# Block 1's softmax attention: two heads of a pair per step, on halves of the TensorE array

## Chip, cores and metric

One core of one Trainium2 chip. The metric is the device time of one launch in microseconds (us); the median of three runs is compared. All data are float32; TensorE runs each float32 matmul as two passes (so the trace counts two for each).

## What is computed

Two transformer-like blocks for 512 tokens of width 1024, then a final norm. Block 1 has two attentions of 8 heads with 64 dimensions each, sigmoid gates, a projection, an output product, and a product-key expert layer that gathers 128 expert rows per token. The change is in the first of these attentions:

```python
def dsa_attention(q, k, v, qi, ki, wi, rel_bias):
    ...
        score = jnp.einsum('bths,bth->bts', rel, wib).astype(jnp.float32) * idx_scale
        ...
        top_score, idx = lax.top_k(score, topk)
        ...
        logits = jnp.einsum('bthd,btkhd->bhtk', qb, kg).astype(jnp.float32) * (dh ** -0.5)
        bias = rel_bias[t5_bucket(q_pos[None, :, None] - idx)].astype(jnp.float32)
        logits = logits + jnp.moveaxis(bias, -1, 1)
        logits = jnp.where(valid[:, None], logits, -jnp.inf)
        p = jax.nn.softmax(logits, axis=-1).astype(v.dtype)
        return jnp.einsum('bhtk,btkhd->bthd', p, vg)
...
merged = jax.nn.sigmoid(ga) * (ya @ w_proj_a[l]) + jax.nn.sigmoid(gb) * (yb @ w_proj_b[l])
```

The kernel does not gather the chosen keys: it keeps all keys up to the query tile and adds a mask (`mask`) for the ones that were not chosen. By then the masks exist, as do q, k and v.

## The kernel before

Every engine has a program of its own, written out by hand, and runs it strictly in order; the engines wait for each other through counting semaphores. A `Signal` has `ready(n)` (item n is done) and `free(n, depth)` (item n - depth is done, so that its place can be used again). No planner orders this part; the order is that of the loops.

Block 1 runs in stages: norm, the q/k products, index scores, the second (stick-breaking) attention with the top-k masks beside it, and then the stage of this change. In it the softmax attention and the 16 gate products are woven into each other. A **unit** n is one head h = n // 4 and one query tile i = n % 4 of 128 tokens, with i + 1 key tiles of 128; there are 32. The gate products are 16 tiles (`S_GATE`) of 24 TensorE products each (lines 627 to 629: the high and low halves of a float32 product, 8 times 3); half a tile goes with each unit.

For a unit, in order:
- TensorE `scores` (L773): queries times keys, 64 rows of the array (rows 0 to 63 for even heads, 64 to 127 for odd), into bank 2 or 3. It waits (`s_taken`) until VectorE has taken the unit that used the bank before.
- VectorE (L1880) adds the bias rows and writes to one of three `logit` buffers; it waits first until the transposes of unit n - 3 have read that buffer (`t_done`). Then L1882 adds the mask and reduces to the row's extreme, and signals `s_taken`.
- ScalarE `exponents` (L1314), VectorE reciprocal of the sum (L1885), ScalarE `normalize` (L1320).
- TensorE `transposes` (L789), one per key tile, into bank 4 or 5; ScalarE `copy_turned` (L1332) copies them to `probT`.
- TensorE `values` (L799), one matmul per key tile, accumulated in a 64-column half of bank 6 or 7.
- When a pair of heads is complete, VectorE copies its y (L1777, L1779) and signals `y_taken`, for which the projection waits.

TensorE's loop (L805 to 813) issues in iteration n: scores(n+1), half a gate tile, transposes(n-1), values(n-2). ScalarE also copies each finished gate tile (L1325) and rounds the weight tile after next (L1202, `high`); VectorE makes that tile's low part (L1743, `low`). SP refills the ring of four weight tiles (L570) whenever TensorE has finished one. The projection (L816 on) starts only after the last y is taken.

Of the kernel before, what the change touches and what calls it, by code (L numbers as in the profile page):

```python
# [4 lines left out]
P = 128  # L5
D = 1024
KT = D // P
T = 512
TT = T // P
META = 16  # L10
L2 = META + T
NH, DH = 8, 64
HP = NH // 2
# [23 lines left out]
S_QK, S_KI, S_WI, S_V, S_GATE = 0, 20, 21, 22, 30  # L37
# [183 lines left out]
def program(nc, xT, metaT, cond, w_ada, small, onehot, rel_bias, w_stream, sub_keys, experts, outT):  # L221
    f32, u32, f32r = mybir.dt.float32, mybir.dt.uint32, mybir.dt.float32r
    ALU, ACT, AX = mybir.AluOpType, mybir.ActivationFunctionType, mybir.AxisListType.X
# [3 lines left out]
    with ctx:  # L227
# [32 lines left out]
        ident = sb("ident", [P, P])  # L260
# [9 lines left out]
        sq = sb("sq", [P, 2, L2])  # L270
        rstd = sb("rstd", [P, L2])
        col = sb("col", [P, 16])
# [39 lines left out]
        masks_at = used[0]  # L312
        mask = [take(P * (i + 1)) for i in range(TT)]
        probT = [take(TT, P) for _ in range(2)]
        logit = [sq[:, 0, 0:T], sq[:, 1, 0:T], take(T)]
        wi_rows = sq[0:NH, 0, 0:T]
        work = used[0]
        bias_rows = take(NH, T)
# [88 lines left out]
        def bank(b, width=512, start=0):  # L407
            return psum[:, b * 512 + start:b * 512 + start + width]
# [202 lines left out]
        def _(pe):  # L611
# [151 lines left out]
                weighted(m)  # L763


            def unit(n):
                return n // TT, n % TT

            def scores(n):
                h, i = unit(n)  # L770
                r = slice(64 * (h % 2), 64 * (h % 2) + 64)
                pe.wait_ge(s_taken.sem, s_taken.free(n, 2))
                mm(bank(2 + n % 2, P * (i + 1)), qk[r, QA + h // 2, i * P:(i + 1) * P],  # L773
                   qk[r, KA + h // 2, 0:P * (i + 1)], start=True, stop=True).then_inc(s_done.sem, 1)

            def half_gate(n):
                g, part_of = n // 2, n % 2
# [7 lines left out]
            def transposes(n):  # L785
                pe.wait_ge(p_done.sem, p_done.ready(n))
                pe.wait_ge(t_taken.sem, t_taken.free(n, 2))
                for j in range(unit(n)[1] + 1):
                    last = nc.tensor.transpose(bank(4 + n % 2, P, j * P), logit[n % 3][:, j * P:(j + 1) * P], ident[:])  # L789
                last.then_inc(t_done.sem, 1)  # L790

            def values(n):
                h, i = unit(n)
                q, e = h // 2, h % 2
                if n % (2 * TT) == 0:
                    pe.wait_ge(y_taken.sem, y_taken.free(q, 2))
                pe.wait_ge(t_taken.sem, t_taken.ready(n))
                for j in range(i + 1):
                    last = mm(bank(6 + q % 2, P, i * P)[64 * e:64 * e + 64, :], v[:, j, h * DH:(h + 1) * DH],  # L799
                              probT[n % 2][:, j, :], start=j == 0, stop=j == i)  # L800
                last.then_inc(pv_done.sem, 1)

            pe.wait_ge(yb_taken.sem, yb_taken.ready(HP - 1))
            scores(0)
            for n in range(NH * TT + 2):  # L805
                if n + 1 < NH * TT:
                    scores(n + 1)
                if n < NH * TT:
                    half_gate(n)
                if 1 <= n <= NH * TT:  # L810
                    transposes(n - 1)
                if n >= 2:
                    values(n - 2)


            pe.wait_ge(y_taken.sem, y_taken.ready(HP - 1))  # L816
# [364 lines left out]
        def _(act):  # L1181
# [14 lines left out]
            def high(n):  # L1196

                act.wait_ge(ring_ready[n % SLOTS], 16 * (n // SLOTS + 1))
                same = n - (4 if S_V + 4 <= n < S_GATE + 2 else 2)
                if same >= 0 and not S_V + 2 <= n < S_V + 4:  # L1200
                    act.wait_ge(tile_done.sem, tile_done.ready(same))
                op(rounded(n), ring[:, n % SLOTS, :], ACT.Copy).then_inc(w_rounded.sem, 1)  # L1202
# [102 lines left out]
                    soft_side(m + 1)  # L1305
                weights(m, 3)

            def unit(n):
                return n // TT, n % TT

            def exponents(n):
                w = P * (unit(n)[1] + 1)
                act.wait_ge(s_taken.sem, s_taken.ready(n))
                op(logit[n % 3][:, 0:w], logit[n % 3][:, 0:w], ACT.Exp, scale=-1.0, bias=col[:, n % 3:n % 3 + 1],  # L1314
                   accum_out=col[:, 3 + n % 3:4 + n % 3]).then_inc(exp_done.sem, 1)

            def normalize(n):
                w = P * (unit(n)[1] + 1)
                act.wait_ge(share_done.sem, share_done.ready(n))
                op(logit[n % 3][:, 0:w], logit[n % 3][:, 0:w], ACT.Copy, scale=col[:, 6 + n % 3:7 + n % 3])\  # L1320
                    .then_inc(p_done.sem, 1)

            def gate(g):
                act.wait_ge(tile_done.sem, tile_done.ready(S_GATE + g))
                op(gates[:, g, :], bank(g % 2), ACT.Copy).then_inc(dense_act.sem, 1)  # L1325

            def copy_turned(n):
                i = unit(n)[1]
                act.wait_ge(t_done.sem, t_done.ready(n))
                if n >= 2:  # L1330
                    act.wait_ge(pv_done.sem, pv_done.ready(n - 2))
                op(probT[n % 2][:, 0:i + 1, :], bank(4 + n % 2, P * (i + 1)).rearrange("p (a b) -> p a b", b=P),  # L1332
                   ACT.Copy).then_inc(t_taken.sem, 1)

            for n in range(NH * TT + 1):
                if n < NH * TT:
                    exponents(n)
                    normalize(n)
                if n % 2 == 1:
                    gate(n // 2)  # L1340
# [367 lines left out]
        def _(dve):  # L1708
# [160 lines left out]
            take_pair(HP - 1)  # L1869

            dve.wait_ge(bias_loaded, 16)
            for n in range(NH * TT + 2):
                if n < NH * TT:
                    h, i = n // TT, n % TT
                    w = P * (i + 1)
                    lg = logit[n % 3][:, 0:w]
# [5 lines left out]
                    V.tensor_tensor_reduce(out=lg, in0=lg, in1=mask[i], scale=1.0, scalar=-TAKEN, op0=ALU.add,  # L1882
                                           op1=ALU.min, accum_out=col[:, n % 3:n % 3 + 1]).then_inc(s_taken.sem, 1)
                    dve.wait_ge(exp_done.sem, exp_done.ready(n))
                    V.reciprocal(col[:, 6 + n % 3:7 + n % 3], col[:, 3 + n % 3:4 + n % 3]).then_inc(share_done.sem, 1)  # L1885
                if n >= 2 and n % 2 == 0:
                    low(S_GATE + n // 2 + 1)
                if n >= 9 and n % 8 == 1:
                    q = n // 8 - 1
                    dve.wait_ge(pv_done.sem, pv_done.ready(8 * q + 7))  # L1890
                    low_part(y_low[0][:, q, :], bank(6 + q % 2), y_high[0][:, q, :])
                    tell(dve, steps, y_taken)


# [373 lines left out]
```

## Time and profile before

| | us |
|---|---|
| median of 3 runs | 2556.46 (2549.74 to 2558.13) |
| the profiled execution: device time | 2555.75 |
| the profiled execution: span of the trace | 2553.8 |
| TensorE busy | 2147.7 (84%) |
| VectorE busy | 1340.0 (52%) |
| ScalarE busy | 932.8 (37%) |
| GpSimd busy | 592.7 (23%) |

In the rows, PE is TensorE, PEld its weight loads, DVE VectorE, ACT ScalarE, POOL GpSimd and SP SyncE; L773 is line 773. `DVEq` is VectorE's sequencer (a semaphore increment by an instruction of its own). PEclk is the TensorE clock that was granted, as a share of the full 2.4 GHz; 0.50 is 1.2 GHz. The span is the time from the first to the last instruction; the device time has some 2 us more around it. TensorE's matmuls are pipelined: the duration of one is longer than the distance to the next, so distances between starts tell what a matmul costs in a stream.

### The profile page before, as it was taken

To read this page: it belongs to the slowest core of one execution; us is meant where nothing else is said; L and a number is where in the kernel's file an instruction comes from. 1 tells how busy PE (TensorE), PEld (TensorE's weight loads), DVE (VectorE), ACT (ScalarE), POOL (GpSimd) and SP (SyncE) were. 2 spreads that over 40 slices of the span, in tenths; PEclk is the share of its full clock that TensorE was granted. 3 is DMA by queue.
4 is the path that set the end of the run, shared out by engine and by line. 5 is a ranking of instruction groups with operands and counts; after the bars stand their busy time and mean duration, and the time that the engine had idled before them with its cause. 6 is when DMAs were issued, how large, how long until landed. Compare 5 with 4: busy or idle time off the path is not lost.

```text
span 2553.8 us, 30169 instructions
## 1 busy us (share of the span) xinstructions
PE 2147.7 (84%) x10876; PEld 1309.5 (51%) x10876; DVE 1340.0 (52%) x3152; ACT 932.8 (37%) x2322; POOL 592.7 (23%) x568
## 2 busy tenths in 40 slices
PE   5999999998878655655566898899999878999999
PEld 3877567776634211111112543356666535668888
DVE  7743754354667777777778677754443342111000
ACT  3124434523334433333334558734443123421000
POOL 0000100000344444444443334433332220000000
PEclk9999999999989877787878998899999999889999
DMA  8821001122799999999999999999999992114454
GB/s 329 293 72 59 1 26 58 58 99 66 299 419 419 421 419 413 421 421 416 416 412 418 377 356 421 379 419 418 418 417 418 418 378 66 42 43 140 156 154 151
DMA packets 124272, 710.48 MB, mean 278 GB/s; under 512 B 14648, under 2 KB 16824, under 8 KB 58464
## 3 DMA queue, kind: packets, MB, share of 16 engines
q0 software_dynamic: 74432, 540.07, 51.5%
q1 hardware_dynamic: 49456, 168.38, 18.9%
q8 instruction: 83, 1.36, 0.2%
q14 instruction: 61, 0.50, 0.1%
q10 hardware_dynamic: 240, 0.16, 0.0%
HBM read 706.45 MB, written 2.12 MB: 277 GB/s over the span
## 4 chain that ended last, share of the span: by engine, by line
PE 57%; DMA 27%; DVE 6%; ACT 5%; issue 3%; POOL 2%; SPq 0%; ACTq 0%; POOLq 0%; DVEq 0%
DMA arena<-experts,eidx 26%; PE psum L1138 9%; PE psum L882 9%; PE psum L627 6%; PE psum L628 5%; PE psum L629 5%; DVE arena L1725 3%; PE psum L1151 3%; POOL arena L1700 2%; PE psum L1120 2%; PE psum L949 2%; PE psum L999 2%; PE psum L739 1%; ACT sq L1406 1%; PE psum L715 1%
## 5 line engine op out<-in xcount | busy, mean ns | idle before, releaser
L882 PE MATMUL psum<-arena,sq 64*64 64x512 f32 x4096 | 626.4, 737 | 333.6 <-ACT sq L1406 326.4
L1725 DVE CUSTOM_DVE_ANT_0 arena<-arena 128x1024 f32<-128x1024 f32 x560 | 679.5, 1223 | 390.9 <-DMA arena<-experts,eidx 360.7
L1700 POOL DMA_INDIRECT arena<-experts,eidx x512 | 577.8, 1128 | 963.8 <-PE psum L882 771.9
L882 PEld LDWEIGHTS psum<-arena,sq 64*64 64x64 f32 x4096 | 152.2, 153 | 725.8 <-ACT sq L1406 503.1
L1138 PE MATMUL psum<-n_t,ring 128*128 128x256 f32 x1408 | 313.9, 382 | 2.4 <-DVE n_t L1722 2.4
L1392 ACT ACTIVATE arena<-arena 128x2 f32<-128x2 f32 x256 | 52.0, 203 | 722.1 <-DVE arena L1725 720.7
L1138 PEld LDWEIGHTS psum<-n_t,ring 128*128 128x128 f32 x1408 | 264.3, 190 | 66.1 <-issue 30.5
L627 PE MATMUL psum<-hn_high,w_high 128*128 128x512 f32 (+1 forms) x432 | 178.6, 413 | 14.6 <-DVE hn_low L1722 13.3
L628 PE MATMUL psum<-hn_low,w_high 128*128 128x512 f32 (+1 forms) x432 | 173.3, 401 | 0.0
L629 PE MATMUL psum<-hn_high,ring_low 128*128 128x512 f32 (+1 forms) x432 | 172.1, 398 | 0.0
L1406 ACT ACTIVATE sq<-sq,arena 128x64 f32<-128x64 f32 x512 | 150.3, 340 | 24.9 <-ACT arena L1398 1.5
L1398 ACT ACTIVATE arena<-arena 128x1 f32<-128x1 f32 x512 | 122.9, 287 | 10.4
L1202 ACT ACTIVATE w_high<-ring 128x1024 fp32r<-128x1024 f32 x74 | 77.9, 1055 | 132.3 <-PE psum L629 130.8
L627 PEld LDWEIGHTS psum<-hn_high,w_high 128*128 128x128 f32 (+1 forms) x432 | 81.8, 189 | 62.3 <-issue 36.2
L1743 DVE TENSOR_TENSOR ring_low<-ring,w_high 128x1024 fp32r<-128x1024 f32 x74 | 90.1, 1219 | 39.4 <-ACT w_high L1202 37.8
L1392 ACT ACT_TABLE_LOAD x75 | 96.2, 1283 | 7.1 <-ACT hn_rest L1618 4.0
L629 PEld LDWEIGHTS psum<-hn_high,ring_low 128*128 128x128 f32 (+1 forms) x432 | 82.1, 190 | 20.0
L628 PEld LDWEIGHTS psum<-hn_low,w_high 128*128 128x128 f32 (+1 forms) x432 | 82.2, 190 | 17.3
L1689 POOL TENSOR_SCALAR_AFFINE_SELECT arena<-arena 128x128 f32<-128x128 f32 x32 | 9.3, 292 | 271.9 <-DVE arena L1722 271.5
L1618 ACT ACTIVATE hn_rest<-psum 128x256 f32<-128x256 f32 x44 | 16.9, 383 | 143.2 <-PE psum L1138 142.9
L1120 PE MATMUL psum<-mix,ring 128*128 128x256 f32 x256 | 59.0, 390 | 2.1 <-ACTq L1502 2.1
L1151 PE MATMUL psum<-w_rest,ring 128*128 128x256 f32 x256 | 59.0, 381 | 0.0
(280 smaller groups left out, 2814.0 us busy)
## 6 DMA issues: line engine op xcount, KB each, us to landing
ring<-w_stream SPq DMA_DIRECT2D x264, 512.0 KB, 4.1
arena<-w_ada SPq DMA_DIRECT2D x48, 512.0 KB, 6.4
arena<-experts,eidx POOLq DMA_INDIRECT x512, 12.4
x<-xT SPq DMA_DIRECT2D x1, 2048.0 KB, 14.9
arena<-rel_rows POOLq DMA_DIRECT2D x1, 2048.0 KB, 15.0
outT<-hn_rest SPq DMA_DIRECT2D x16, 128.0 KB, 6.0
arena<-sub_keys POOLq DMA_DIRECT2D x1, 1024.0 KB, 6.3
arena<-cond SPq DMA_DIRECT2D x1, 512.0 KB, 4.4
```

The costliest lines, as they stand in the source:

```text
L627: mm(out, a[0], b[0], start=start, stop=False)
L628: mm(out, a[0], b[1], start=False, stop=False)
L629: return mm(out, a[1], b[0], start=False, stop=stop)
L882: last = mm(bank(4 + 2 * odd + a)[HALF * b:HALF * b + HALF, :], diag[k, s, :], rows[k, s, D + a * 512:D + (a + 1) * 512], start=c == 0, st ...
L1120: last = mm(bank(b, PAIR), w[:, k, :], mix[:, k, :], start=k == 0, stop=k == KT - 1)
L1138: last = mm(bank(b, PAIR), w[:, k, :], n_t[:, k, 0:PAIR], start=k == 0, stop=k == KT - 1)
L1151: last = mm(bank(b, PAIR), w[:, f % 8, :], act_ff[f], start=f == 0, stop=f == FF - 1)
L1392: steps(op(pre[:, s:s + 2], pre[:, s:s + 2], ACT.Gelu))
L1398: steps(op(coef[:, s + c:s + c + 1], pre[:, s + c:s + c + 1], ACT.Copy, scale=wgt[:, n // P % 2, k:k + 1]))
L1406: op(diag[:, s + c, :], ident_pair, ACT.Copy, scale=coef[:, s + c:s + c + 1]).then_inc(diag_done.sem, 1)
L1700: nc.gpsimd.indirect_dma_start(rows[:, s, :], None, experts, bass.IndirectOffsetOnAxis(ap=eidx[:, n // P % 2, n % P:n % P + 1], axis=0)).t ...
L1725: return V.tensor_tensor_reduce(out=out, in0=a, in1=b, scale=1.0, scalar=0.0 if op1 == ALU.add else TAKEN, op0=op0, op1=op1, accum_out=accum)
```

## The change

A **step** s now is one pair of heads q = s // 4 and one query tile i = s % 4, so two units, 2s (even head) and 2s + 1 (odd head); there are 16 steps. TensorE issues the two scores matmuls one after the other, on rows 0 to 63 and 64 to 127 of the array and into banks 2 and 3, and alternates the values of the two heads, which go to columns 0 to 63 and 64 to 127. Each step has a whole gate tile, in two halves with the values between them. The order within an iteration is scores(s+1), first half of the gate tile, values(s-2), second half, transposes(s-1). There are four `logit` buffers in place of three, and the small columns beside them move accordingly. ScalarE and VectorE do the two units of a step one after the other, operation by operation.

```diff
-        logit = [sq[:, 0, 0:T], sq[:, 1, 0:T], take(T)]
+        logit = [sq[:, 0, 0:T], sq[:, 1, 0:T], take(T), take(T)]
...
-            def scores(n):
-                h, i = unit(n)
-                r = slice(64 * (h % 2), 64 * (h % 2) + 64)
-                pe.wait_ge(s_taken.sem, s_taken.free(n, 2))
-                mm(bank(2 + n % 2, P * (i + 1)), qk[r, QA + h // 2, i * P:(i + 1) * P],
-                   qk[r, KA + h // 2, 0:P * (i + 1)], start=True, stop=True).then_inc(s_done.sem, 1)
+            def scores(s):
+                q, i = s // TT, s % TT
+                pe.wait_ge(s_taken.sem, s_taken.free(2 * s + 1, 2))
+                for e in range(2):
+                    r = slice(64 * e, 64 * e + 64)
+                    mm(bank(2 + e, P * (i + 1)), qk[r, QA + q, i * P:(i + 1) * P], qk[r, KA + q, 0:P * (i + 1)],
+                       start=True, stop=True).then_inc(s_done.sem, 1)
...
+            def transposes(s):
+                for e in range(2):
+                    n = 2 * s + e
+                    pe.wait_ge(p_done.sem, p_done.ready(n))
+                    pe.wait_ge(t_taken.sem, t_taken.free(n, 2))
+                    for j in range(s % TT + 1):
+                        last = nc.tensor.transpose(bank(4 + e, P, j * P), logit[n % 4][:, j * P:(j + 1) * P], ident[:])
+                    last.then_inc(t_done.sem, 1)
+
+            def values(s):
+                q, i = s // TT, s % TT
+                if i == 0:
                     pe.wait_ge(y_taken.sem, y_taken.free(q, 2))
+                pe.wait_ge(t_taken.sem, t_taken.ready(2 * s + 1))
                 for j in range(i + 1):
+                    for e in range(2):
+                        h = 2 * q + e
+                        last = mm(bank(6 + q % 2, P, i * P)[64 * e:64 * e + 64, :], v[:, j, h * DH:(h + 1) * DH],
+                                  probT[e][:, j, :], start=j == 0, stop=j == i)
+                        if j == i:
+                            last.then_inc(pv_done.sem, 1)
...
             scores(0)
-            for n in range(NH * TT + 2):
-                if n + 1 < NH * TT:
-                    scores(n + 1)
-                if n < NH * TT:
-                    half_gate(n)
-                if 1 <= n <= NH * TT:
-                    transposes(n - 1)
-                if n >= 2:
-                    values(n - 2)
+            S = HP * TT
+            for s in range(S + 2):
+                if s + 1 < S:
+                    scores(s + 1)
+                if s < S:
+                    half_gate(s, 0)
+                if s >= 2:
+                    values(s - 2)
+                if s < S:
+                    half_gate(s, 1)
+                if 1 <= s <= S:
+                    transposes(s - 1)
```

On ScalarE:

```diff
-            for n in range(NH * TT + 1):
-                if n < NH * TT:
-                    exponents(n)
-                    normalize(n)
-                if n % 2 == 1:
-                    gate(n // 2)
-                if n >= 1:
-                    copy_turned(n - 1)
-                if n % 2 == 1:
-                    high(S_GATE + n // 2 + 2)
+            S = HP * TT
+            for s in range(S + 1):
+                if s < S:
+                    exponents(2 * s)
+                    exponents(2 * s + 1)
+                    normalize(2 * s)
+                    normalize(2 * s + 1)
+                    gate(s)
+                if s >= 1:
+                    copy_turned(2 * s - 2)
+                    copy_turned(2 * s - 1)
+                if s < S:
+                    high(S_GATE + s + 2)
```

On VectorE:

```diff
+            for s in range(S + 2):
+                q, i = s // TT, s % TT
+                w = P * (i + 1)
+                for n in (2 * s, 2 * s + 1) if s < S else ():
+                    lg = logit[n % 4][:, 0:w]
                     dve.wait_ge(s_done.sem, s_done.ready(n))
-                    if n >= 3:
-                        dve.wait_ge(t_done.sem, t_done.ready(n - 3))
-                    steps(V.tensor_tensor(lg, bank(2 + n % 2, w), bias_rows[:, h, 0:w][:, ::-1], ALU.add))
+                    if n >= 4:
+                        dve.wait_ge(t_done.sem, t_done.ready(n - 4))
+                    steps(V.tensor_tensor(lg, bank(2 + n % 2, w), bias_rows[:, 2 * q + n % 2, 0:w][:, ::-1], ALU.add))
                     steps.wait()
...
+                for n in (2 * s, 2 * s + 1) if s < S else ():
                     dve.wait_ge(exp_done.sem, exp_done.ready(n))
...
-                if n >= 2 and n % 2 == 0:
-                    low(S_GATE + n // 2 + 1)
+                if 1 <= s <= S:
+                    low(S_GATE + s + 1)
+                if s >= 5 and s % 4 == 1:
+                    y_of = s // 4 - 1
+                    dve.wait_ge(pv_done.sem, pv_done.ready(8 * y_of + 7))
```

## Rows read from the trace of the kernel before

**Rows 1.** The page, part 4: shares of the span in the chain that ended last.
```profile
PE 57%; DMA 27%; DVE 6%; ACT 5%; issue 3%; POOL 2%; SPq 0%; ACTq 0%; POOLq 0%; DVEq 0%
```

**Rows 2.** Windows, stage and four units: length; busy PE, PEld, DVE, ACT, POOL; PEclk; DMA; GB/s.
```profile
347.16:499.29 152.13, 150.04 (x689) 105.93 (x689) 58.47 (x152) 75.78 (x162) 0.00 (x0) 1.00 0.18 56
378.31:397.05 18.74, 18.74 (x88) 13.25 (x87) 6.33 (x17) 9.01 (x21) 0.00 (x0) 1.00 0.19 57
```

**Rows 3.** Chain that ended last, 405 to 412 us: start, length, what.
```profile
405.02 0.44 PE psum L789 x4
405.46 0.80 PE psum L799 x6
406.26 0.84 PE psum L773 x2
407.10 0.43 PE psum L627
408.23 0.24 PE psum L628
...
410.21 1.02 PE psum L799 x8
411.23 1.05 PE psum L773 x2
```

**Rows 4.** Timeline of TensorE, one expert combine: start, length; in brackets the idle time before.
```profile
2106.46 1.95 PE L882 MATMUL psum<-arena,sq 64*64 64x512 f32 x16 [1.64 <-ACT sq L1406]
```

**Rows 5.** Timeline of VectorE: first and last instruction of two units' taking.
```profile
399.69 0.29 DVE L1880 TENSOR_TENSOR sq<-psum,arena 128x128 f32<-128x128 f32 x1
400.23 0.08 DVE L1882 DVE_READ_ACCUMULATOR2_ANT col<- 128x1 f32 x1
...
413.68 0.68 DVE L1880 TENSOR_TENSOR sq<-psum,arena 128x512 f32<-128x512 f32 x1
...
415.01 0.08 DVE L1882 DVE_READ_ACCUMULATOR2_ANT col<- 128x1 f32 x1
```

**Rows 6.** Timeline of the end of the stage, from the last gate product on.
```profile
493.43 0.39 PE L629 MATMUL psum<-hn_high,ring_low 128*128 128x512 f32 x1
...
493.86 0.60 ACT L1325 ACTIVATE arena<-psum 128x512 f32<-128x512 f32 x1 [1.30 <-PE psum L629]
...
494.35 0.48 ACT L1332 ACTIVATE arena<-psum 128x384 f32<-128x384 f32 x1
...
497.45 0.69 DVE L1777 CAST ya_high<-psum 128x512 fp32r<-128x512 f32 x1 [0.41 <-PE psum L799]
...
499.29 0.49 PE L627 MATMUL psum<-ya_high,w_high 128*128 128x512 f32 x1 [1.88 <-DVEq L552]
```

**Rows 7.** Timeline: the stage's start, and three more pauses of TensorE.
```profile
347.16 0.92 PE L773 MATMUL psum<-arena 64*128 64x128 f32 x4 [1.64 <-DVEq L552]
347.76 0.29 DVE L1880 TENSOR_TENSOR sq<-psum,arena 128x128 f32<-128x128 f32 x1 [0.70 <-PE psum L773]
...
549.13 0.79 PE L627 MATMUL psum<-merged_high,w_high 128*128 128x512 f32 x1 [3.42 <-DVEq L552]
...
2126.05 3.69 PE L926 MATMUL psum<-n_t,mean_ones 128*128 128x256 f32 x16 [2.16 <-ACT n_t L1425]
...
2287.85 3.41 PE L1120 MATMUL psum<-mix,ring 128*128 128x256 f32 x9 [2.10 <-ACTq L1502]
```

**Rows 8.** Windows of TensorE around these pauses: length, PE busy, PEclk, DMA, GB/s.
```profile
345.50:352.50 7.00, 5.36 (x22) 1.00 0.00 0
497.40:504.40 7.00, 5.12 (x16) 0.76 0.00 0
545.70:552.70 7.00, 3.58 (x9) 0.65 0.65 226
2124.00:2131.00 7.00, 3.69 (x16) 1.00 0.00 0
2285.80:2292.80 7.00, 4.95 (x15) 0.76 0.25 75
```

More of the change, by code:

```diff
@@ L763, in _, with half_gate @@
                 weighted(m)
-            def unit(n):
-                return n // TT, n % TT
-            def scores(n):
-                h, i = unit(n)
-                r = slice(64 * (h % 2), 64 * (h % 2) + 64)
-                pe.wait_ge(s_taken.sem, s_taken.free(n, 2))
-                mm(bank(2 + n % 2, P * (i + 1)), qk[r, QA + h // 2, i * P:(i + 1) * P],
-                   qk[r, KA + h // 2, 0:P * (i + 1)], start=True, stop=True).then_inc(s_done.sem, 1)
-            def half_gate(n):
-                g, part_of = n // 2, n % 2
+            def scores(s):
[5 more added lines that the diff above has]
+                       start=True, stop=True).then_inc(s_done.sem, 1)
+            def half_gate(g, part_of):
                 w = tile(S_GATE, g)
@@ L783, in half_gate @@
                     last.then_inc(tile_done.sem, 1)
[L785 to L795, printed above, removed]
+            def transposes(s):
[6 more added lines that the diff above has]
+                    last.then_inc(t_done.sem, 1)
@@ L796, in values @@
+            def values(s):
+                q, i = s // TT, s % TT
+                if i == 0:
                     pe.wait_ge(y_taken.sem, y_taken.free(q, 2))
-                pe.wait_ge(t_taken.sem, t_taken.ready(n))
+                pe.wait_ge(t_taken.sem, t_taken.ready(2 * s + 1))
                 for j in range(i + 1):
-                    last = mm(bank(6 + q % 2, P, i * P)[64 * e:64 * e + 64, :], v[:, j, h * DH:(h + 1) * DH],
-                              probT[n % 2][:, j, :], start=j == 0, stop=j == i)
@@ L801, in values @@
-                last.then_inc(pv_done.sem, 1)
+                    for e in range(2):
[4 more added lines that the diff above has]
+                            last.then_inc(pv_done.sem, 1)
             pe.wait_ge(yb_taken.sem, yb_taken.ready(HP - 1))
             scores(0)
-            for n in range(NH * TT + 2):
-                if n + 1 < NH * TT:
-                    scores(n + 1)
-                if n < NH * TT:
-                    half_gate(n)
-                if 1 <= n <= NH * TT:
-                    transposes(n - 1)
-                if n >= 2:
-                    values(n - 2)
+            S = HP * TT
@@ L1306, in _ @@
                 weights(m, 3)
-            def unit(n):
-                return n // TT, n % TT
             def exponents(n):
-                w = P * (unit(n)[1] + 1)
+                w = P * (n // 2 % TT + 1)
                 act.wait_ge(s_taken.sem, s_taken.ready(n))
-                op(logit[n % 3][:, 0:w], logit[n % 3][:, 0:w], ACT.Exp, scale=-1.0, bias=col[:, n % 3:n % 3 + 1],
-                   accum_out=col[:, 3 + n % 3:4 + n % 3]).then_inc(exp_done.sem, 1)
+                op(logit[n % 4][:, 0:w], logit[n % 4][:, 0:w], ACT.Exp, scale=-1.0, bias=col[:, n % 4:n % 4 + 1],
+                   accum_out=col[:, 4 + n % 4:5 + n % 4]).then_inc(exp_done.sem, 1)
             def normalize(n):
-                w = P * (unit(n)[1] + 1)
+                w = P * (n // 2 % TT + 1)
                 act.wait_ge(share_done.sem, share_done.ready(n))
-                op(logit[n % 3][:, 0:w], logit[n % 3][:, 0:w], ACT.Copy, scale=col[:, 6 + n % 3:7 + n % 3])\
+                op(logit[n % 4][:, 0:w], logit[n % 4][:, 0:w], ACT.Copy, scale=col[:, 8 + n % 4:9 + n % 4])\
                     .then_inc(p_done.sem, 1)
@@ L1327, in copy_turned @@
             def copy_turned(n):
-                i = unit(n)[1]
+                i = n // 2 % TT
                 act.wait_ge(t_done.sem, t_done.ready(n))
@@ L1871, in _ @@
             dve.wait_ge(bias_loaded, 16)
[L1872 to L1876, printed above, removed]
+            S = HP * TT
+            for s in range(S + 2):
[3 more added lines that the diff above has]
+                    lg = logit[n % 4][:, 0:w]
                     dve.wait_ge(s_done.sem, s_done.ready(n))
-                    if n >= 3:
-                        dve.wait_ge(t_done.sem, t_done.ready(n - 3))
-                    steps(V.tensor_tensor(lg, bank(2 + n % 2, w), bias_rows[:, h, 0:w][:, ::-1], ALU.add))
+                    if n >= 4:
+                        dve.wait_ge(t_done.sem, t_done.ready(n - 4))
+                    steps(V.tensor_tensor(lg, bank(2 + n % 2, w), bias_rows[:, 2 * q + n % 2, 0:w][:, ::-1], ALU.add))
@@ L1881, in _ @@
                     steps.wait()
                     V.tensor_tensor_reduce(out=lg, in0=lg, in1=mask[i], scale=1.0, scalar=-TAKEN, op0=ALU.add,
-                                           op1=ALU.min, accum_out=col[:, n % 3:n % 3 + 1]).then_inc(s_taken.sem, 1)
+                                           op1=ALU.min, accum_out=col[:, n % 4:n % 4 + 1]).then_inc(s_taken.sem, 1)
+                for n in (2 * s, 2 * s + 1) if s < S else ():
                     dve.wait_ge(exp_done.sem, exp_done.ready(n))
-                    V.reciprocal(col[:, 6 + n % 3:7 + n % 3], col[:, 3 + n % 3:4 + n % 3]).then_inc(share_done.sem, 1)
@@ L1886, in _ @@
-                if n >= 2 and n % 2 == 0:
-                    low(S_GATE + n // 2 + 1)
[L1888 to L1891, printed above, removed]
+                    V.reciprocal(col[:, 8 + n % 4:9 + n % 4], col[:, 4 + n % 4:5 + n % 4]).then_inc(share_done.sem, 1)
+                if 1 <= s <= S:
+                    low(S_GATE + s + 1)
@@ L1892, in _ @@
+                if s >= 5 and s % 4 == 1:
+                    y_of = s // 4 - 1
+                    dve.wait_ge(pv_done.sem, pv_done.ready(8 * y_of + 7))
+                    low_part(y_low[0][:, y_of, :], bank(6 + y_of % 2), y_high[0][:, y_of, :])
                     tell(dve, steps, y_taken)
```

## The prediction

> **What bounds the kernel now.** I read the page first, then one stage of it, then the order of work inside that stage. The chain that ended last is TensorE for 57% of the span and DMA for 27% [rows 1]; the DMA share belongs to the expert gathers, which come later. The change touches one stage only, block 1's softmax attention, from the first scores matmul at 347.16 us to the first product of the projection at 499.29 us. In those 152.13 us TensorE is busy for 150.04 at full clock, VectorE for 58.47, ScalarE for 75.78 [rows 2]. So TensorE's own queue sets this stage; what it saves or waits there moves all that follows, because projection, queries and gathers each start on what came before. The other engines have room for their sums, but only if nobody in the queue has to wait for them.
>
> The stage holds 32 units (8 heads, 4 query tiles), of 1, 2, 3 and 4 key tiles in turn, and 16 gate tiles of 24 products. The chain prices a unit [rows 3]: a transposed tile 0.11 us (0.44 for four); values of three tiles 0.80 and of four 1.02, so 0.14 + 0.22 per tile; scores of three tiles 0.84 and of four 1.05, so 0.20 + 0.21 per tile; the first gate product behind a scores matmul 0.43 against 0.23 to 0.24 later, so 0.20 more. These small constants are what a change of the array's shape costs. A check: four units have 10 tiles each of transposes (1.10), values (2.76) and scores (2.92), 4 x 0.20 behind the scores, and 48 gate products of 0.2325 (11.16): 18.74 us, which is exactly the period from 378.31 to 397.05 [rows 2].
>
> **What the change saves on TensorE.** A step now handles both heads of a pair. The two scores matmuls use row halves 0 to 63 and 64 to 127 and write banks 2 and 3; the two chains of values use column halves. Before shows no such pair side by side in this stage. The nearest row is the expert combine, which puts 64 x 64 quarters side by side: 16 matmuls of 512 columns in 1.95 us at full clock [rows 4], where sixteen in a row at the 0.43 of a scores pass (0.85 for two) would need 6.8. That is all four quarters at work together. So I take a pair at the price of one, in full. The bounds are this and no overlap at all. Transposes stay as they are. Changes of shape fall: scores and values now each have gate products on both sides, which costs 2 x 0.20 per step behind them, where two units had 2 x 0.20 as well, while the 0.14 and 0.20 are paid once and not twice. Four steps (8 units) thus take 22.32 for gates, 2.20 for transposes, 2.76 for values, 2.92 for scores and 8 x 0.20: 31.80 us against 37.48. Over 16 steps that is **-22.7 us**. Without any overlap, 0.21 and 0.22 times 40 tiles come back (17.2 us), and -5.5 is left.
>
> The Trainium skill ("TensorE: Matmul & The Clock Gate", Part 3, The mechanism) says that matmuls start and end strictly in program order and overlap only across different tiles of the array. As each of these matmuls is two passes on the same tile, a pair would by that rule need three slots and not two for scores, and the sum would come out about 6 us higher. The combine's 1.95 us does not agree with it: with two passes in order on each quarter, at most two would run together.
>
> **What the change makes TensorE wait for.** VectorE turns a unit's scores into logits in two operations (L1880, L1882), and writes them into a logit buffer that must have been transposed. Before, three buffers for single units leave room: unit n waits for the transposes of unit n-3, issued an iteration or more before anybody needs the result. Now four buffers are two steps. Step s+1 writes where step s-1 was, and the transposes of step s-1 are the last thing in TensorE's iteration s. The first thing in iteration s+1 is scores(s+2), which waits until both units of step s+1 are taken from banks 2 and 3. So TensorE finishes the transposes, VectorE then does two adds and two reductions, and only then can TensorE go on. Both gate halves, the values and the next transposes stand behind that wait in the queue. Nothing covers it.
>
> Its size: one unit takes VectorE 0.62 us for one key tile (399.69 to 400.31) and 1.41 for four (413.68 to 415.09) [rows 5], so 0.62 + 0.263 per further tile. Two units with a gap of 0.05 take 1.29, 1.82, 2.34 and 2.87. From the end of a TensorE stream to the start of the engine that waits for it I take 0.20 (gate product 493.43 + 0.23, gate copy 493.86) [rows 6], and 0.05 back to TensorE. TensorE still streams the second head's transposes meanwhile, 0.11 per tile of step s-1 (3, 4, 1 and 2 tiles), and 0.10 of the scores' constant falls inside the wait. The waits are 1.29+0.25-0.33-0.10 = 1.11, 1.82+0.25-0.44-0.10 = 1.53, then 2.34+0.25-0.11-0.10 = 2.38, and 2.87+0.25-0.22-0.10 = 2.80 us for steps of 1, 2, 3 and 4 key tiles. They occur for VectorE's steps 3 to 15, in all 13: 4 x 2.80 + 3 x (1.11 + 1.53 + 2.38) = **+26.3 us**. This is the price of the operations alone; a late VectorE would add to it. I find no lateness: its reciprocals, its weight tile (1.2 us) and the y part (1.4 us) are done in the middle of TensorE's iteration.
>
> Smaller terms. At the start, scores(1) waits for both units of step 0; VectorE starts at 347.76 [rows 7], ends the pair at 349.05, TensorE goes on at 349.10 instead of 347.57: **+1.5**. At the end, before has 5.63 us from the last gate product (493.66) to 499.29, of which 3.2 are transposes and values: 2.5 bare. After: transposes(14), gate copy until +0.80, two copies of 0.48, values(14) until +2.6, transposes(15) until +3.6, two four-tile copies of 0.60 (the form of the gate copy) until +4.45, values(15) until +5.65, then the same 1.84 of VectorE and signal as from 497.45 to 499.29 [rows 6]: 7.5, of which 3.4 is TensorE's work, 4.1 bare: **+1.7**. ScalarE's exponents, normalisations and copies cost nothing more: after a wait it needs about 6 us to the last normalisation, TensorE comes to the next transposes after about 10. If that cover went, each us would be paid 13 times. SP's ring refills are released by the same gate tiles, 16 in some 150 us; POOL does nothing here. The sum at full clock is -22.7 + 26.3 + 1.5 + 1.7 = **+6.8 us**.
>
> **The clock.** The stage runs at 1.00 now, with no pause in it. The new pauses are 1.1 to 2.8 us long. Pauses of this length in the trace go both ways [rows 7, 8]: after 1.64 us (347.16) and 2.16 us (2126.05) the mean clock of the 7 us around stays 1.00; after 1.88 us (499.29) [rows 6] and 2.10 us (2287.85) it is 0.76; after 3.42 us it is 0.65. One fall to 1.2 GHz thus costs 0.24 x 7 = 1.7 us. I take six falls in thirteen, near the two of four: **+10.2 us**. The bounds are none (0) and all thirteen (+22). The tail's fall is there before and after.
>
> The Trainium skill ("TensorE: Matmul & The Clock Gate", Why this matters for your kernels) warns only of idle gaps longer than any that I expect here; by it none of these would cost clock and the forecast would be the second case below. The trace does not agree: the 1.88 us pause was followed by 0.76.
>
> **Forecast.** +6.8 + 10.2 = +17.0. Against the profiled execution's own 2555.75 us (span 2553.8) this is 2572.8; that execution lies 0.7 us under the median of the runs, 2556.46, so the median gives 2573.5. I say **2573 us, slower, chance 0.60**. A measurement can tell about 0.3%, 7.7 us, from no change.
>
> **The rivals.**
> Clock holds: the waits are as computed but the pauses cost no clock. +6.8, so 2563 us. For it: two pauses of four above. Chance 0.20, on the border of what can be told, so 0.13 goes to no change and 0.07 to slower.
> Pairs do not overlap: the halves run one after another, so that the change does not do what it says. 17.2 more than the forecast: 2590 us. Against it [rows 4]; for it, that no row has row halves or column halves alone. Chance 0.10, all slower; the in-order rule of the skill lies between the two.
> Faster: TensorE's wait for the two logit units decides. If VectorE takes the pair soon enough after the first head's transposes, the 22.7 us stay. The place is the head of iterations 2 to 14; the point from which it decides is a mean wait of (22.7 - 1.5 - 1.7) / 13 = 1.5 us with the clock up, against my 2.0. With no wait there at all the time would be 2556.5 - 19.5 = 2537 us. For it: TensorE saves more than in any other place of the stage, and VectorE is busy only 38% of it. Against it: the order of signals, in which no other work can slip in. Chance 0.10, of which 0.02 lands within 0.3%.
>
> **The numbers.** Faster 0.08, same 0.15, slower 0.77 (0.60 + 0.07 + 0.10). The range runs from under the clock-holds case, 2558, to the no-overlap case, 2591; it leaves out the faster case, and more than six falls on top of no overlap.
>
> **What would show it.** In the profile after: scores matmuls as groups of four with an idle time before them, put down to VectorE, 13 times, of 1.1 to 2.8 us by the step's width; a group of two three-tile scores at 0.84 and not 1.5; VectorE's add waiting for the transposes; the stage's length at 347 to about 523 us; its mean clock near 0.94 instead of 1.00. Wrong: no idle time before the scores, or a stage under 152 us; a paired scores group twice as long; a clock at 1.00.

## The result, and the profile after

The changed kernel takes 2566.9 us (median of 20 runs, 2555.94 to 2574.51), the kernel before 2554.77 (20 runs, 2544.61 to 2559.97): 12.1 us more, ratio 1.0049 with a 95% interval of 1.0037 to 1.0060. The profiled execution took 2571.63 us against 2555.75, 15.9 us more. It lies 4.7 us above its kernel's median. Single executions differ outside this stage too: in the nine profiles of this document the stage begins at 345.2 to 352.3 us, and what follows it, which is the same code in all, takes 2042.0 to 2058.0 us. So what the profiles are compared by below is the length of the stage.

The first view is the window of the stage, from its first scores matmul to the first product of the projection; the columns are those of [rows 2].

```profile
347.10:515.09 167.99, 138.77 (x689) 99.42 (x689) 58.76 (x152) 71.25 (x162) 0.00 (x0) 0.93 0.16 51
```
Against the 152.13 us of before [rows 2] the stage begins at the same time and is 15.9 us longer. From its end to the end of the span both kernels take the same (2569.7 - 515.09 = 2054.6, 2553.8 - 499.29 = 2054.5 us). So between these two executions all of the difference is here. VectorE and ScalarE are busy about as long as before (58.76 against 58.47 us, 71.25 against 75.78). TensorE is busy for 11 us less, idle for 27 us more, and its mean clock is 0.93 and no longer 1.00.

The second view is TensorE's timeline with what is idle before the scores of eight steps, and one group of values:

```profile
366.04 2.08 PE L771 MATMUL psum<-arena 64*128 64x512 f32 x4 [2.28 <-DVE col L1887]
378.19 0.49 PE L771 MATMUL psum<-arena 64*128 64x128 f32 x4 [2.71 <-DVE col L1887]
388.45 0.70 PE L771 MATMUL psum<-arena 64*128 64x256 f32 x4 [1.00 <-DVE col L1887]
398.24 0.92 PE L771 MATMUL psum<-arena 64*128 64x384 f32 x4 [1.42 <-DVE col L1887]
402.06 1.09 PE L799 MATMUL psum<-arena 128*64 128x128 f32 x16
408.67 1.13 PE L771 MATMUL psum<-arena 64*128 64x512 f32 x4 [2.28 <-DVE col L1887]
419.26 0.49 PE L771 MATMUL psum<-arena 64*128 64x128 f32 x4 [2.71 <-DVE col L1887]
...
483.29 0.92 PE L771 MATMUL psum<-arena 64*128 64x384 f32 x4 [1.42 <-DVE col L1887]
...
493.75 1.13 PE L771 MATMUL psum<-arena 64*128 64x512 f32 x4 [2.28 <-DVE col L1887]
```

The scores of a single unit of four key tiles in the kernel before, and a pair after, each with the gate product that follows:

```profile
411.16 1.12 PE L773 MATMUL psum<-arena 64*128 64x512 f32 x2
412.21 0.51 PE L627 MATMUL psum<-hn_high,w_high 128*128 128x512 f32 x1
...
449.76 1.13 PE L771 MATMUL psum<-arena 64*128 64x512 f32 x4 [2.28 <-DVE col L1887]
450.82 0.50 PE L627 MATMUL psum<-hn_high,w_high 128*128 128x512 f32 x1
```

Two things are to be seen. A scores pair of four key tiles (x4: two matmuls of two passes each) takes 1.13 us where a single unit had taken 1.12, and the gate product follows its start after 1.06 us, as against 1.05 before. Both heads' values of four key tiles, sixteen passes, take 1.09, as long as the eight of one head alone (e5 below). The halves of the array do work side by side. And ahead of each of the last thirteen scores pairs TensorE now stands idle for 1.0, 1.4, 2.3 or 2.7 us, released by VectorE. The waits within the stage add it up (us in total, times, longest):

```profile
DVE arena L1885 <- PE psum L788: 42.0, 7, 7.3
DVE sq L1885 <- PE psum L788: 30.3, 7, 8.2
PE psum L771 <- DVE col L1887: 25.8, 14, 2.7
```

VectorE's add (L1885) waits for the transposes (L788), TensorE's scores (L771) for VectorE's reduction (L1887). The chain shows one such turn, without anything between its links (start, length):

```profile
406.17 0.23 PE psum L788 x2
406.40 0.55 DVE sq L1885
...
407.46 0.08 DVE col L1887
407.54 0.48 DVE sq L1885
408.02 0.02 issue
408.05 0.56 DVE sq L1887
408.61 0.02 DVE col L1887
408.62 0.04 issue
408.67 1.13 PE psum L771 x4
```

The clock is seen in windows of TensorE (length, busy, PEclk, DMA, GB/s), the first two around the pause that ends at 366.04, the others around the one that ends at 378.19:

```profile
361.00:366.04 5.04, 2.76 (x13) 0.99 0.26 81
366.04:370.04 4.00, 4.00 (x10) 0.58 0.09 33
375.00:379.00 4.00, 1.29 (x11) 1.00 0.42 131
379.00:384.00 5.00, 5.00 (x21) 0.66 0.00 0
```

In the stage of this execution TensorE fell to 1.2 GHz six times, five times with a loss of 1.7 us of full-speed time and once of 3.2, 11.6 us in all (windows of 1 us, 1 - PEclk times TensorE's busy time, summed up). The first of the six comes right after the start of the stage, where a pause of 1.32 us follows one of 1.63:

```profile
347.06 0.49 PE L771 MATMUL psum<-arena 64*128 64x128 f32 x4 [1.63 <-DVEq L552]
348.87 1.22 PE L771 MATMUL psum<-arena 64*128 64x256 f32 x4 [1.32 <-DVE col L1887]
```

A fall right behind the stage is there in both kernels, at 500 us before and at 516 us after.

### The profile page after: what moved, and what is told of

It reads as the page before. It is cut to its first block, busy times and chain, and to the rows that moved or that the text cites. A ratio compares the mean times of both kernels' runs of the same rounds, so it can differ in the third digit from the quotient of the medians.

```text
span 2569.7 us, 30168 instructions
## 1 busy us (share of the span) xinstructions
PE 2134.7 (83%) x10876; PEld 1300.1 (51%) x10876; DVE 1340.0 (52%) x3152; ACT 928.4 (36%) x2322; POOL 597.1 (23%) x568
## 4 chain that ended last, share of the span: by engine, by line
PE 57%; DMA 26%; DVE 6%; ACT 6%; issue 3%; POOL 2%; ACTq 0%; SPq 0%; POOLq 0%; DVEq 0%
DMA arena<-experts,eidx 25%; PE psum L1142 10%; PE psum L886 9%; PE psum L627 6%; PE psum L628 5%; PE psum L629 5%; DVE arena L1729 3%; PE psum L1155 3%; POOL arena L1704 2%; PE psum L953 2%; PE psum L1003 2%; PE psum L1124 2%; PE psum L739 1%; ACT sq L1410 1%; PE psum L715 1%
## 5 line engine op out<-in xcount | busy, mean ns | idle before, releaser
L1124 PE MATMUL psum<-mix,ring 128*128 128x256 f32 x256 | 57.4, 382 | 2.1 <-ACTq L1506 2.1
L1155 PE MATMUL psum<-mix,ring 128*128 128x256 f32 x256 | 59.0, 381 | 0.0
```

Source lines behind the costliest of these rows:

```text
L1124: last = mm(bank(b, PAIR), w[:, k, :], mix[:, k, :], start=k == 0, stop=k == KT - 1)
L1155: last = mm(bank(b, PAIR), w[:, f % 8, :], act_ff[f], start=f == 0, stop=f == FF - 1)
```

## The experiments

**e1, six logit buffers.** The wait's reason is taken away and TensorE's order left alone. The sixth buffer is the place of the index keys, which nobody reads by then.

```diff
-        logit = [sq[:, 0, 0:T], sq[:, 1, 0:T], take(T), take(T)]
+        logit = [sq[:, 0, 0:T], sq[:, 1, 0:T], take(T), take(T), take(T), ki[:]]
...
-                    if n >= 4:
-                        dve.wait_ge(t_done.sem, t_done.ready(n - 4))
+                    if n >= 6:
+                        dve.wait_ge(t_done.sem, t_done.ready(n - 6))
```
(and `n % 6` for `n % 4` wherever `logit` is indexed)

> Edit: six logit buffers instead of four, so that VectorE's step s+1 waits for the transposes of step s-2 and no longer for those that TensorE has just issued; the order of TensorE's work is untouched. Theory (the wait for the logit buffers sets TensorE's pauses): the idle time before the scores matmuls, 25.8 us in 14 places after the change, falls under 4 us (what is left is at the start), the clock stays at 1.00 through the stage, the stage takes 168.0 - 24.5 - about 12 = 131 to 134 us against 152.1 before, and the kernel about 2536 us, ratio to before 0.992 to 0.994. Rival (pairing costs TensorE or ScalarE something of its own, for instance ScalarE comes late when it does two units at a time): pauses remain before transposes or values, the stage stays above 145 us and the kernel within 8 us of before.

Measured: 2533.0 us (4 runs), ratio 0.9914 (0.9892 to 0.9937). The profiled execution is the slowest of the four (2543.03), and its stage begins 5 us later than before's; only the stage is compared. It is:

```profile
352.30:488.23 135.93, 128.92 (x688) 93.67 (x689) 58.15 (x152) 70.45 (x162) 0.00 (x0) 0.99 0.20 63
```

32 us shorter than after the change, by the buffers alone. Ten of the thirteen pauses are gone. The one at the start stays (1.32 us, with one fall of the clock), and three of 0.75 to 0.77 us are left where VectorE takes a pair's y first:

```profile
397.68 0.69 DVE L1781 CAST ya_high<-psum 128x512 fp32r<-128x512 f32 x1 [0.97 <-PE psum L799]
...
398.40 0.69 DVE L1783 TENSOR_TENSOR ya_low<-psum,ya_high 128x512 fp32r<-128x512 f32 x1
...
399.31 0.56 DVE L1885 TENSOR_TENSOR sq<-psum,arena 128x384 f32<-128x384 f32 x1 [0.21 <-DVE ya_low L1783]
...
401.59 1.13 PE L771 MATMUL psum<-arena 64*128 64x512 f32 x4 [0.76 <-DVE col L1887]
```

VectorE waits 0.97 us for the values, does 1.4 us for y, and begins the step's adds late. My expectation of 131 to 134 us left these three and the fall out (2.3 and 1.7 us). The theory stands, and the rival that pairing costs something of its own falls.

**e2, scores behind the first half gate tile.** The wait stays, work is put over it.

```diff
+                if s < S:
+                    half_gate(s, 0)
                 if s + 1 < S:
                     scores(s + 1)
-                if s < S:
-                    half_gate(s, 0)
                 if s >= 2:
                     values(s - 2)
```

> Edit: in TensorE's iteration the first half of the gate tile goes ahead of scores(s+1); everything else as in the change. Theory: VectorE has the 2.8 us of the half tile to take the pair (it needs 1.0 to 2.7 beyond TensorE's own transposes), so that all 13 pauses go; scores directly ahead of values also save one change of the array's shape per step (about 0.2 us). Stage about 130 us, clock 1.00, kernel about 2533 us, ratio 0.991 to 0.993. Rival (the pauses only move: scores(s+1) issued 2.8 us later makes VectorE or ScalarE late for the transposes): idle time of over 10 us in the stage, put down to ScalarE, and a kernel time above 2545.

Measured: 2526.23 us (5 runs), ratio 0.9892 (0.9873 to 0.9911). The stage, and one scores pair and values within it:

```profile
345.30:473.36 128.06, 124.66 (x688) 92.11 (x689) 58.79 (x152) 71.28 (x162) 0.00 (x0) 1.00 0.22 66
```
```profile
400.61 0.49 PE L771 MATMUL psum<-arena 64*128 64x128 f32 x4
401.03 0.66 PE L799 MATMUL psum<-arena 128*64 128x128 f32 x8
```

No pause stands before any scores pair, no fall lies in the stage, and what idle time is left (3.4 us) is in the tail, behind ScalarE's copies and VectorE's y. The rival falls. This version beats both kernels, before by 1.1%. Part of that is not the pauses: the change's stage without its falls, the 24.5 us and the start's 1.3 would be 130.6 us, and 2.5 less are left here, with scores directly ahead of values (expected: about 0.2 us per step).

**e3, the pauses filled.** It takes the clock apart from the wait.

```diff
             for s in range(S + 2):
+                if 2 <= s < S - 1:
+                    w = tile(S_GATE, s)
+                    pe.wait_ge(dense_act.sem, dense_act.free(A_GATE + s, 2))
+                    for _ in range((4, 6, 9, 11)[s % 4]):
+                        mm(bank(s % 2), w[0][:, 0, :], rhs[0][:, 0, :], start=True, stop=True)
                 if s + 1 < S:
                     scores(s + 1)
```

> Edit: ahead of the scores of iterations 2 to 14 TensorE does 4, 6, 9 or 11 products of 128 x 512 that nobody reads, 0.93, 1.40, 2.10 and 2.56 us of work, as long as the pauses there (1.00, 1.42, 2.28, 2.71). Nothing else is computed otherwise. Theory (a third of the loss is the clock): the waits keep their end, so no us is gained on them, but the clock stays at 1.00 and the five falls inside the stage go: about 10 us less than the change, 2557 us, ratio to before about 1.001. Rival (the falls cost nothing on the path, or come from elsewhere): the kernel stays at 2567 us, ratio 1.005, with the same lower clock in the stage.

Measured: 2561.42 us (12 runs, 2553.11 to 2571.43), ratio 1.0029 (1.0016 to 1.0042). The stage:

```profile
347.80:506.71 158.91, 152.53 (x787) 111.01 (x788) 58.78 (x152) 71.30 (x162) 0.00 (x0) 0.99 0.17 54
```

The pauses shrink to 0.2 us at most. In the stage only the fall after the start is left, and the stage is 9.1 us shorter than in the change's first profile, 6.2 shorter than in its second (e7), though TensorE does 99 products more. The rival falls in the traces. Over the timed runs the gain is 5.5 us, about half of what I gave, but the two intervals (1.0016 to 1.0042, 1.0037 to 1.0060) overlap a little: an estimate from their widths puts the gain anywhere between about 1 and 9 us. So the clock's part is real in the traces; how large it is over many executions, the timed runs do not settle.

**e4, adds first.** Half of the wait is taken away.

```diff
-                pe.wait_ge(s_taken.sem, s_taken.free(2 * s + 1, 2))
+                pe.wait_ge(s_read.sem, s_read.free(2 * s + 1, 2))
...
                     steps(V.tensor_tensor(lg, bank(2 + n % 2, w), bias_rows[:, 2 * q + n % 2, 0:w][:, ::-1], ALU.add))
-                    steps.wait()
+                for n in (2 * s, 2 * s + 1) if s < S else ():
+                    lg = logit[n % 4][:, 0:w]
+                    if n % 2 == 0:
+                        steps.wait()
+                        dve.sem_inc(s_read.sem, 2)
```
(`s_read` is a new signal)

> Edit: VectorE does both adds of a step first and then signals that banks 2 and 3 are read; the two reductions follow. TensorE's scores wait for that signal. Half of the suspected wait is taken away, its place stays. Theory: pauses of about 0.5, 0.6, 1.2 and 1.3 us in place of 1.0, 1.4, 2.3 and 2.7, together about 12 us instead of 24.5, hardly a fall of the clock, kernel 2543 to 2550 us, ratio 0.996 to 0.998. Rival (what TensorE waits for is something other than VectorE's two operations): pauses as after the change, kernel about 2567 us.

Measured: 2545.05 us (10 runs), ratio 0.9961 (0.9944 to 0.9979). The pauses:

```profile
364.87 1.13 PE L772 MATMUL psum<-arena 64*128 64x512 f32 x4 [1.14 <-DVEq L1891]
374.06 0.49 PE L772 MATMUL psum<-arena 64*128 64x128 f32 x4 [1.29 <-DVEq L1891]
382.29 0.70 PE L772 MATMUL psum<-arena 64*128 64x256 f32 x4 [0.51 <-DVEq L1891]
391.30 0.92 PE L772 MATMUL psum<-arena 64*128 64x384 f32 x4 [0.64 <-DVEq L1891]
```

The thirteen sum up to 12.2 us, as computed from VectorE's adds (one, before the scores at 427.26, is 0.91 and not 0.64), and none of them is followed by a fall. One fall comes after the start, where the pause is now 0.70 us; the stage is 145.95 us. Half the wait is gone and the kernel is 22 us faster than the change. Without the falls the stages are 144.2 and 156.4 us, so 12.2 are the wait itself; by the profiles the rest is the clock (1.7 us lost in the stage against 11.6).

**e5, the pairs taken apart.** Against e2: the same operations, but the even head's scores and values stand behind the first half gate tile and the odd head's behind the second. The last two values have no gate products between them, so there the heads follow each other directly.

```diff
                 if s < S:
                     half_gate(s, 0)
                 if s + 1 < S:
-                    scores(s + 1)
+                    scores(s + 1, (0,))
                 if s >= 2:
-                    values(s - 2)
+                    values(s - 2, (0,))
                 if s < S:
                     half_gate(s, 1)
+                if s + 1 < S:
+                    scores(s + 1, (1,))
+                if s >= 2:
+                    values(s - 2, (1,))
```
(the second argument of `scores` and `values` says which heads are issued)

> Edit against e2 (scores after the first half gate tile): the even head's scores and values stand after the first half gate tile, the odd head's after the second, so that no two halves of the array are side by side; every engine does the same operations. Theory (pairing saves what one of two streams takes): 0.21 and 0.22 us times 40 key tiles come back, 17 us, and two more changes of shape per step, about 0.35 us times 16, 5 us; the stage goes from 128.1 to about 150 us, the kernel from 2526 to 2548 us, ratio about 0.997. Rival (the pairs' overlap is worth little, and e2's gain came from the order of the work): below 2535 us, a stage under 137 us.

Measured: 2552.39 us (10 runs), ratio 1.0000 (0.9985 to 1.0016). The stage:

```profile
345.20:499.23 154.03, 148.36 (x689) 102.74 (x689) 58.54 (x152) 74.11 (x163) 0.00 (x0) 1.00 0.17 55
```

26.0 us longer than e2's, of which 2.4 are three pauses of 0.79 before four-tile scores. Another 0.8 lie in the last two values, which stand head by head and take 1.15 and 1.58 us where they took 0.88 and 1.09 in e2. The other 22.8 are what pairing is worth at this place: by the prices of [rows 3] 15.4 of streams side by side (39 key tiles of scores, 33 of values), which leaves 7.4 for changes of the array's shape that are not paid a second time (0.49 us in each of 15 steps; I had given 0.35). One head's four key tiles of values, eight passes, take as long as both heads' sixteen in the change:

```profile
396.75 1.09 PE L799 MATMUL psum<-arena 128*64 128x128 f32 x8
```

Without pairing, the new order gains nothing over before that the runs could tell (ratio 1.0000). So the 1.1% of e2 is the pairing, within the intervals.

**e6, values head by head.** Against the change: the loops over heads and key tiles are swapped.

```diff
-                for j in range(i + 1):
-                    for e in range(2):
+                for e in range(2):
+                    for j in range(i + 1):
```

> Edit against the change: values issues all key tiles of the even head and then all of the odd head, in place of alternating. Theory (the halves of the array work from the queue independently, whatever stands between two matmuls of one half): sixteen passes of four key tiles still take 1.09 us, the stage is as long as after the change. Rival (matmuls start in the order of the queue): the odd head's start when the even head's last has started, sixteen take about 1.09 + 0.75 us, and values cost 16 steps x 0.2 to 0.75 us more, 8 us in all.

Measured: 2577.39 us (one run); the stage is 169.23 us, 159.3 without the falls, against 156.4 of the change. Three groups of values at full clock, of two, three and four key tiles:

```profile
467.77 0.67 PE L799 MATMUL psum<-arena 128*64 128x128 f32 x8
...
476.67 1.14 PE L799 MATMUL psum<-arena 128*64 128x128 f32 x12
...
486.91 1.58 PE L799 MATMUL psum<-arena 128*64 128x128 f32 x16
```

With alternating heads they take 0.66, 0.88 and 1.09; with one head alone after the other, at 0.22 us per key tile [rows 3], they would take 0.66 + 0.44, 0.88 + 0.66 and 1.09 + 0.88. Neither theory holds. With four passes of each head the order costs nothing (0.01 us). With six and eight the odd head does start before the even head's last pass, but not at once: the groups are 0.26 and 0.49 us longer, about 2.4 and 4.5 passes of 0.11 us, where a queue without any order would give 0. Four times the three differences is 3.0 us, and the stage without its falls is 2.9 longer. In all three cases it is as if the odd head could start once three to four passes of the even head are left. That would fit a TensorE that looks only so far ahead in its queue; this mechanism is argued from the three lengths, and no run tests it. The last two values of e5, in the same order, take the same 1.15 and 1.58.

**e7, the change again.** The same kernel, a second profile.

> The changed kernel itself, for a second profile. The pauses ahead of the scores are the same to 0.02 us (1.00, 1.42, 2.28, 2.71). Theory (whether a pause of 2.3 or 2.7 us lets the clock fall differs from execution to execution): another set of pauses is followed by a fall, their number is anything from 2 to 7, and the stage's length differs from 168.0 by 1.7 us for each. Rival (a pause of a given place always does the same): the same six falls, the one at 461 us twice as long, and a stage of 168.0.

Measured: 2565.9 us (one run). The pauses are the same to 0.01 us; the stage:

```profile
347.70:512.84 165.14, 135.91 (x689) 96.91 (x689) 58.80 (x152) 71.33 (x162) 0.00 (x0) 0.95 0.16 51
```

Five falls of 1.7 us and no long one, 8.5 us in all against 11.6. They do not come at the same places: the pause that ends at 378.84 is followed by none here, where in the first profile the same pause is, and the one at 407.80 is, where in the first it was not. The rival falls.

## Why the prediction was right

The forecast was 2573 us, slower, 17.0 us over before; measured are 2566.9 by the median, 12.1 over before, and 2571.63 in the profiled execution, both within the range. The forecast stood on a median of before of 2556.46 from three runs; over 20 runs it is 2554.77. Its steps, one by one:

- **What the pairs save**: predicted 22.7 us. The stage of 168.0 us less 11.6 for the clock is 156.4, 4.3 more than before. Less the waits of 24.5 and 1.3 and the tail's 1.4, this makes 22.9. TensorE's busy time says the same: 138.77 less 11.6 for the clock is 127.2, against 150.04 before. (The prediction's check of its prices was a little less exact than it says: ten tiles of scores at 0.20 + 0.21 make 2.90 and not 2.92, and the period 18.72 and not 18.74.) The taking of a pair at the price of one was right for scores (1.13 us against 1.12) and for values (1.09 for both heads and for one alone), and e5 takes the same thing away from the other side.
- **The wait for the logit buffers**: predicted 1.11, 1.53, 2.38 and 2.80, together 26.3; measured 1.00, 1.42, 2.28 and 2.71, together 24.5. The 0.1 us too much in each lies in the 0.20 that I took from a gate copy: in the chain above the transpose starts at 406.17, streams for 0.11, and VectorE's add starts at 406.40, 0.12 us later. The count was off by one step as well. The prediction has the waits at VectorE's steps 3 to 15, four of them with four key tiles; they occur at steps 2 to 14, ahead of scores 3 to 15, and four of them are those with three. By its own prices that is 25.8 us. That this wait and nothing else is the reason is shown by e1 (reason away, pauses away), e4 (half the work, half the pauses) and e2 (work over it).
- **Start and tail**: predicted 1.5 and 1.7. Measured is an idle time of 1.32 at the start. In the tail it is 7.2 us from the end of the last gate product's stream (507.64 + 0.23) to 515.09, where I had 7.5, so 1.4 and not 1.7.
- **The clock**: predicted 10.2 us, six falls in thirteen pauses. The first profile has six, one of them double, 11.6 us; the second five, 8.5. But one fall in each stands behind the start, which I had not counted among the thirteen, so that the number six came out partly by luck. By the medians, 24.5 - 22.9 + 1.3 + 1.4 = 4.3 us are there at full clock, where the forecast had 6.8, and 12.1 measured leave about 8 for the clock. The interval of the ratio makes that 5 to 11, so the 10.2 are not excluded, and no more is e3's 5.5. So about half of the 4.9 us too much lies in the waits and the smaller terms, and the rest, if it is more than noise, in the clock. "Half of all pauses" was the wrong shape: the falls come after the long ones, as the last section tells.
- **The rivals**: the case without overlap is excluded by the rows above. The clock-holds case (2563 us) is by time alone nearer to the median of 2566.9 than the forecast is; it is the falls in both profiles that exclude it, not the time. The faster case asked for a mean wait under 1.5 us. With 1.9 us (24.5 / 13) the change lost; with 0.94 (12.2 / 13) in e4 it wins 0.4%, and with none it wins 1.1% (e2).

So the change brought what it meant to bring, and gave it back in a new wait. The fourth logit buffer was not enough to keep the slack. Three buffers for single units are three items deep, and the transposes that VectorE needed were long past; four buffers for pairs are only two steps deep, and the transposes are the work just before the scores that wait.

The rule of the Trainium skill that matmuls start strictly in program order, which the prediction set against the combine's row ("TensorE: Matmul & The Clock Gate", Part 3, The mechanism), would have cost about 6 us in sum. The pairs as the change issues them do not show it: two passes of each half, issued one half after the other, take the time of one half (1.13 us against 1.12). e6 shows that there is something in it all the same, once six or eight passes of one half stand ahead in the queue (1.14 us against 0.88, 1.58 against 1.09).

What stays open: why a given pause is or is not followed by a fall; how many falls a median execution has, as both profiles of the change are single executions; and why the rest of the kernel, the same code, takes 2042.0 us in one profile and 2058.0 in another.

## What to carry to other kernels

Before work is regrouped so that two items go at a time, count the buffers in steps and not in items, and look in every engine's queue at what stands directly ahead of the instruction that waits. A ring through two engines (here transposes, then VectorE's adds and reductions, then scores) cost its full length once per step, because its two ends were neighbours in one queue. The cheapest cure is often to move the waiting instruction behind work that is there anyway: one exchange of two lines turned +0.5% into -1.1%. Small matmuls on different halves of the array should stand next to each other (22.8 us of the stage in e5) and alternate (2.9 us in e6).

## What the runs showed of the hardware

- Two matmuls on row halves, and two chains on column halves, cost what one costs (1.13 us for two four-tile scores, 1.09 for both heads' values), when the halves alternate. With eight passes of one half ahead of eight of the other it is 1.58, with six 1.14 in place of 0.88, with four 0.67 in place of 0.66.
- In three profiles (the change twice, e6) fourteen of the twenty-one pauses of 2.28 or 2.71 us were followed by a fall of TensorE to 1.2 GHz, and none of the eighteen of 1.00 or 1.42 us. In e4 none of thirteen of 0.51 to 1.29 us was. The start of the stage is another case: a pause of 0.70 (e4) or 1.32 us, with 0.5 us of scores between it and one of 1.63 to 1.64, was followed by a fall in five of six profiles; the pause of 1.63 or 1.64 alone was not in any of three (before, e2, e5). So the length of the last pause alone does not tell. A fall costs 1.7 us of full-speed time, twice 3.2. Over the twenty-one pauses that is 1.3 us each, about half of the pause itself, as a second price.
- The same pause in the same kernel differs in this from execution to execution: the 2.28 us ahead of the scores at 408 us was followed by a fall in the second profile and not in the first. The spread of the timed runs cannot be put down to it. It is 18.6 us for the change, but 15.4 us for before, whose stage has no pause inside (3.3 us for e2, 5 runs only).
